# Who multiplies the one-hots of a key search, and another order in a cross-attention

## The reference, cut to what matters

```python
def memory_cross_attention(h, mem_n, wq, wkv, wo):      # 4 heads of 256, 256 memory rows
    ...
    sc = jnp.einsum('bshd,bmhd->bhsm', q, k)
    p = jax.nn.softmax(sc / math.sqrt(XA_HEAD_DIM), axis=-1)
    o = jnp.einsum('bhsm,bmhd->bshd', p, v)
    return o.reshape(b_, s_, D_MODEL) @ wo

def peer_ffn(x, wq, keys, u_tab, v_tab):                # 8 heads, 128 keys twice, 16384 experts
    q = (xt @ wq).reshape(t, PEER_HEADS, 2, HALF_Q)
    scores = jnp.einsum('thpd,hpnd->thpn', q, keys)
    s_top, i_top = lax.top_k(scores, PEER_TOPK)         # 16 of 128, for each head and half
    cand = (s_top[:, :, 0, :, None] + s_top[:, :, 1, None, :]).reshape(t, PEER_HEADS, 256)
    c_score, c_idx = lax.top_k(cand, PEER_TOPK)         # 16 of 256
    i1 = jnp.take_along_axis(i_top[:, :, 0], c_idx // PEER_TOPK, axis=-1)
    i2 = jnp.take_along_axis(i_top[:, :, 1], c_idx % PEER_TOPK, axis=-1)
    expert = i1 * N_KEYS + i2
    ...                                                 # gelu(x . u[expert]) * gate, then times v[expert]
```

## Time and profile before

| | us |
|---|---|
| median of 3 runs | 1758.8 |
| lowest and highest | 1757.88, 1760.15 |
| the profiled execution, whole | 1758.06 |
| its span, first to last instruction | 1756.3 |
| TensorE busy in it | 1695.2 |
| VectorE busy | 1173.5 |
| ScalarE busy | 932.6 |
| GpSimd busy | 134.0 |

### The profile page before, as it was taken

One profiled execution on the slowest core, in us unless ns is written; L12 is line 12 of the kernel. 1 busy time (PEld: TensorE's weight loads), 2 busy tenths in 40 slices (PEclk: granted clock), 3 DMA queues, 4 the chain that ended last, 5 costly groups with the idle time before them and its releaser, 6 DMA issues.

```text
span 1756.3 us, 30291 instructions
## 1 busy us (share of the span) xinstructions
PE 1695.2 (97%) x10344; PEld 1513.8 (86%) x10344; DVE 1173.5 (67%) x1753; ACT 932.6 (53%) x1536; POOL 134.0 (8%) x109
## 2 busy tenths in 40 slices
PE   7999999989998999999989989899999999999998
PEld 6888898889886788879889989899999988888887
DVE  5555787587654555467654899978888866666664
ACT  5445636476644444456444434456666655554454
POOL 0000004000000000010010020313222200000000
PEclk9999999989998999999999999999999999999999
DMA  7555544223552555544354446353444456555663
GB/s 258 188 182 183 173 169 153 99 96 133 168 170 94 169 189 182 191 157 160 118 188 147 168 143 191 132 166 134 143 139 136 155 179 192 193 192 193 194 194 121
DMA packets 78814, 286.79 MB, mean 163 GB/s; under 512 B 8864, under 2 KB 9120, under 8 KB 78624
## 3 DMA queue, kind: packets, MB, share of 16 engines
q1 hardware_dynamic: 77888, 282.27, 48.2%
q0 software_dynamic: 864, 3.67, 0.6%
HBM read 284.86 MB, written 1.05 MB: 163 GB/s over the span
## 4 chain that ended last, share of the span: by engine, by line
PE 85%; DVE 11%; ACT 3%; issue 1%; DMA 0%; POOL 0%; SPq 0%; ACTq 0%; DVEq 0%; POOLq 0%
PE ps L1698 25%; PE ps L1700 25%; PE ps L1699 25%; PE ps L2253 3%; DVE w_low L989 3%; DVE digit_hot L1593 1%; ACT w_high L483 1%; PE ps L1705 1%; PE ps L1787 1%; PE ps L2084 1%; DVE route L1598 0%; DVE xT_low L1023 0%; DVE tmp L1074 0%; ACT xn L499 0%; PE ps L2219 0%
## 5 line engine op out<-in xcount | busy, mean ns | idle before, releaser
L989 DVE TENSOR_TENSOR w_low<-ring,w_high 128x1024 fp32r<-128x1024 f32 x532 | 654.2, 1233 | 346.3 <-ACT w_high L483 344.4
L483 ACT ACTIVATE w_high<-ring 128x1024 fp32r<-128x1024 f32 x532 | 559.4, 1056 | 322.6 <-PE ps L1700 314.2
L1698 PE MATMUL ps<-xT_high,w_high 128*128 128x256 f32 x1600 | 463.5, 290 | 12.8 <-DVE w_low L989 10.7
L1699 PE MATMUL ps<-xT_high,w_low 128*128 128x256 f32 x1600 | 455.3, 285 | 0.0
L1700 PE MATMUL ps<-xT_low,w_high 128*128 128x256 f32 x1600 | 455.1, 284 | 0.0
L1698 PEld LDWEIGHTS ps<-xT_high,w_high 128*128 128x128 f32 x1600 | 309.7, 194 | 16.0 <-DVE w_low L989 14.0
L1699 PEld LDWEIGHTS ps<-xT_high,w_low 128*128 128x128 f32 x1600 | 309.8, 194 | 0.7 <-issue 0.5
L1700 PEld LDWEIGHTS ps<-xT_low,w_high 128*128 128x128 f32 x1600 | 309.3, 193 | 0.0
L1698 PE MATMUL ps<-w_high,expert_w_high 128*128 128x512 f32 x512 | 199.3, 389 | 0.0
L1699 PE MATMUL ps<-w_high,expert_w_low 128*128 128x512 f32 x512 | 199.2, 389 | 0.0
L1700 PE MATMUL ps<-w_low,expert_w_high 128*128 128x512 f32 x512 | 199.2, 389 | 0.0
(11 more groups left out here) (361 smaller groups left out, 2115.0 us busy)
## 6 DMA issues: line engine op xcount, KB each, us to landing
ring<-in_stream SPq DMA_DIRECT2D x532, 512.0 KB, 3.4
row_gain<-in_rows POOLq DMA_DIRECT2D x4, 512.0 KB, 4.4
h<-in_x SPq DMA_DIRECT2D x2, 512.0 KB, 4.0
mem_sb<-in_mem SPq DMA_DIRECT2D x1, 1024.0 KB, 11.4
keys_sb<-in_keys POOLq DMA_DIRECT2D x1, 1024.0 KB, 5.3
out<-result SPq DMA_DIRECT2D x2, 512.0 KB, 2.6
last_gain<-in_rows POOLq DMA_DIRECT2D x1, 512.0 KB, 5.6
cols<-in_cols SPq DMA_DIRECT2D x1, 78.5 KB, 7.2
```

The source lines that it names most:

```text
L483: act.activation(WH[:, n % SLOTS, :], RING[:, n % SLOTS, :], ACT.Copy).then_inc(w_high, 1)
L989: dve.tensor_tensor(WL[:, n % SLOTS, :], RING[:, n % SLOTS, :], WH[:, n % SLOTS, :].bitcast(F32), ALU.subtract).then_inc(w_split, 1)
L1698: pe.matmul(out, high, w_hi, start=start, stop=False, skip_group_check=True)
L1699: pe.matmul(out, low, w_hi, start=False, stop=False, skip_group_check=True)
```

## The change

In the cross-attention TensorE turns the probabilities between blocks 2 and 3 of kv3. The lower half goes to banks 2 and 3, the upper half to banks 6 and 7. After block 3 it waits for the lower half's copy alone, forms feature tiles 0 to 3 (banks 2 and 3), then waits for the upper half's copy and for kv3 out of PSUM, and forms tiles 4 to 7 (banks 0 and 1). The output product's first four blocks each wait only for the low part that they read. ScalarE and VectorE split two blocks of xa_o, copy their half of `xa_probsT`, split one, copy kv3 out, split the last.

In the key search the key numbers are kept as bfloat16 (`top_at_16`), VectorE itself multiplies both one-hots (line 1601 of the changed kernel), and sums them at once for either tt; GpSimd keeps only the fills. The gate subtraction moves ahead of the one-hots.

```diff
@@ gpsimd
-        for tt in range(TT):
-            if tt:
-                pool.wait_ge(tops_ok, 2)
-                pool.memset(GE[:, FIRST_GATED:80, :], 1.0).then_inc(slots_one, 1)
-            for p in range(2):
-                pool.wait_ge(hot_one, 2 * tt + p + 1)
-                hot = HOT[:, p, :, :].rearrange("p (h k) j -> p h k j", h=8)
-                pool.tensor_tensor(hot, hot, TOP_ATF[:, tt, p:16:2, :].unsqueeze(2).to_broadcast([P, 8, 16, 16]),
-                                   ALU.mult).then_inc(hot_ok, 1)
+        pool.wait_ge(tops_ok, 2)
+        pool.memset(GE[:, FIRST_GATED:80, :], 1.0).then_inc(slots_one, 1)
+        pool.wait_ge(hot_one, 4)
         pool.memset(GE[:, 80:105, :], 1.0).then_inc(slots_one, 1)
@@ scalar, cross-attention
-        split(BASE["xa_o"], 4)
+        split(BASE["xa_o"], 2)
+        act.wait_ge(xp_ps, 1)
+        act.activation(PT[:, 0:4, :], XP_PS[0], ACT.Copy).then_inc(xp_sb, 1)
+        split(BASE["xa_o"] + 2, 1)
         kv_evac(3)
-        act.wait_ge(xp_ps, 1)
-        act.activation(PT[:, 0:4, :], XT_PS[:, 0:4, :], ACT.Copy).then_inc(xp_sb, 1)
+        split(BASE["xa_o"] + 3, 1)
@@ vector, cross-attention
-        split(BASE["xa_o"], 4)
+        split(BASE["xa_o"], 2)
+        dve.wait_ge(xp_ps, 2)
+        dve.tensor_copy(PT[:, 4:8, :], XP_PS[1]).then_inc(xp_upper, 1)
+        split(BASE["xa_o"] + 2, 1)
         kv_evac(3)
-        dve.wait_ge(xp_ps, 2)
-        dve.tensor_copy(PT[:, 4:8, :], XT_PS[:, 4:8, :]).then_inc(xp_sb, 1)
+        split(BASE["xa_o"] + 3, 1)
@@ vector, key search
+            dve.tensor_tensor(gate_of(tt), CTOP[:, tt, :, :], CTOP[:, tt, :, 0:1].to_broadcast([P, 8, 16]),
+                              ALU.subtract).then_inc(gd_ok, 1)
             if tt:
                 dve.wait_ge(hot_used, 2 * tt)
             for p in range(2):
...
                                   ALU.is_equal).then_inc(hot_one, 1)
                 tick(long=True)
+            for p in range(2):
+                dve.wait_ge(hot_one, 2 * tt + p + 1)
+                hot = HOT[:, p, :, :].rearrange("p (h k) j -> p h k j", h=8)
+                dve.tensor_tensor(hot, hot, TOP_AT16[:, tt, p:16:2, :].unsqueeze(2).to_broadcast([P, 8, 16, 16]),
+                                  ALU.mult).then_inc(hot_ok, 1)
+            tick(long=True)
+            keys_of(tt)
@@ tensor, cross-attention
-        kv_panel(3, range(1, 4))
-        kv_out(3)
+        kv_panel(3, range(1, 3))
         for half in range(2):
             for h in (2 * half, 2 * half + 1):
                 for tt in range(TT):
...
             last.then_inc(xp_ps, 1)
-        pe.wait_ge(xp_sb, 2)
+        kv_panel(3, range(3, 4))
+        pe.wait_ge(xp_sb, 1)
         for ft in range(8):
+            if ft == 4:
+                pe.wait_ge(xp_upper, 1)
+                kv_out(3)
...
+        for kt in range(4):
+            pe.wait_ge(xo_low, kt // 2 + 1)
+            rows_product("xa_o", 8, range(kt, kt + 1))
         pe.wait_ge(xo_low, 4)
-        rows_product("xa_o", 8, range(4))
```

More of the change, by code:

```diff
@@ L121, in build @@
     KV_PAIR = [PAIR[1], PAIR[1], PS[:, 2048:3072], PAIR[0]]
+    XP_PS = [p.rearrange("p (k t) -> p k t", k=4) for p in (PAIR[1], PS[:, 3072:4096])]
+    XO_PS = [PS[:, b * 512:(b + 1) * 512] for b in (2, 3, 0, 1)]
     IDENT = sb("ident", [P, P], 64)
@@ L208, in build @@
     HOT = sb("digit_hot", [P, 2, 128, 16], 64.5, BF16)
-    TOP_ATF = sb("top_at_f", [P, TT, 16, 16], 72.5)
+    TOP_AT16 = sb("top_at_16", [P, TT, 16, 16], 72.5, BF16)
     CTOP = sb("cand_top", [P, TT, 8, 16], 74.5)
@@ L313, in build @@
     xs_sc, xs_max, xs_exp, xs_norm = sem("xa_scores"), sem("xa_max"), sem("xa_exp"), sem("xa_norm")
+    xp_upper = sem("xa_probsT_upper_ok")
     xp_ps, xp_sb, xo_ps, xo_high, xo_low = (sem("xa_probsT_psum"), sem("xa_probsT_ok"), sem("xa_o_psum"),
@@ L770, in _ @@
             act.activation(HTH[:, 2 * bank:2 * bank + 2, :],
-                           PS[:, 2048 + bank * 512:2560 + bank * 512].rearrange("p (k t) -> p k t", k=2),
-                           ACT.Copy).then_inc(xo_high, 1)
+                           XO_PS[bank].rearrange("p (k t) -> p k t", k=2), ACT.Copy).then_inc(xo_high, 1)
         act.preload_act_table_set("sqrt_and_others")
@@ L1363, in _ @@
             k2 = slice(2 * bank, 2 * bank + 2)
-            dve.tensor_tensor(HTL[:, k2, :], PS[:, 2048 + bank * 512:2560 + bank * 512].rearrange("p (k t) -> p k t", k=2),
+            dve.tensor_tensor(HTL[:, k2, :], XO_PS[bank].rearrange("p (k t) -> p k t", k=2),
                               HTH[:, k2, :].bitcast(F32), ALU.subtract).then_inc(xo_low, 1)
@@ L1565, in keys_of @@
         def keys_of(tt):
-            dve.wait_ge(hot_ok, 2 * tt + 2)
             for p in range(2):
+                dve.wait_ge(hot_ok, 2 * tt + p + 1)
                 dve.reduce_sum(ROUTE[:, tt, p, :], HOT[:, p, :, :], AX_X).then_inc(hot_used, 1)
@@ L1576, in _ @@
             dve.wait_ge(injected, 1)
-            dve.tensor_copy(TOP_ATF[:, tt, :, :], TOP_AT[:, tt, :, :]).then_inc(tops_ok, 1)
+            dve.tensor_copy(TOP_AT16[:, tt, :, :], TOP_AT[:, tt, :, :]).then_inc(tops_ok, 1)
             chain(dve.tensor_tensor(CAND[:, tt, :, :].rearrange("p h (a b) -> p h a b", a=16),
@@ L1596, in _ @@
                 tick(long=True)
-            dve.tensor_tensor(gate_of(tt), CTOP[:, tt, :, :], CTOP[:, tt, :, 0:1].to_broadcast([P, 8, 16]),
-                              ALU.subtract).then_inc(gd_ok, 1)
-        keys_of(1)
+            for p in range(2):
[5 more added lines that the diff above has]
+            keys_of(tt)
         split(b + PB + ticks[1], STEP0 - ticks[1])
@@ L2077, in _ @@
                     for mt in range(2):
-                        last = pe.transpose(XT_PS[:, 2 * h + mt, tt * P:(tt + 1) * P],
+                        last = pe.transpose(XP_PS[half][:, 2 * h + mt - 4 * half, tt * P:(tt + 1) * P],
                                             PE_[:, tt, h, mt * P:(mt + 1) * P], IDENT[:])
             last.then_inc(xp_ps, 1)
-        pe.wait_ge(xp_sb, 2)
+        kv_panel(3, range(3, 4))
+        pe.wait_ge(xp_sb, 1)
         for ft in range(8):
+            if ft == 4:
+                pe.wait_ge(xp_upper, 1)
+                kv_out(3)
             for mt in range(2):
-                last = pe.matmul(PS[:, 2048 + ft * SEQ:2048 + (ft + 1) * SEQ],
+                last = pe.matmul(XO_PS[ft // 2][:, ft % 2 * SEQ:(ft % 2 + 1) * SEQ],
                                  XAV[:, ft // 4, mt, ft % 4 * P:ft % 4 * P + P], PT[:, ft // 2 * 2 + mt, :],
```

2 lines of the change are left out of this document (removed).

## The result

| | before | changed |
|---|---|---|
| median, us | 1759.5 | 1731.1 |
| lowest and highest, us | 1757.88, 1762.31 | 1729.96, 1734.61 |
| executions | 4 | 4 |
| the profiled execution, us | 1758.06 | 1730.03 |
| mean granted clock in it | 0.985 | 0.991 |

The ratio is 0.984, with a 95% interval from 0.982 to 0.9861: 1.6% faster. Predicted were 1734.1 us, range 1730.5 to 1741.0.

The account below looks back on a forecast made before the run. TensorE, busy 1695.2 of 1756.3 us, bounds the kernel; only its idle and half-clock time can be won. Key search 16.0 plus cross-attention 8.7 gives 24.7 us: 1758.8 - 24.7 = 1734.1, range 1730.5 to 1741.

Parts of the forecast that it names:

- The search, 16.0 us: Key search: without GpSimd's multiplies holding VectorE, idle time and half clock together win 16.0 us, at worst 12.7.
- The multiply, taken from the split's row: Key search: VectorE's new bfloat16 multiply costs 1.15 us net, like a split, within a span of 1.2 to 2.3.
- The row of line 1013: Profile row of 1024 elements in a mean of 0.76 us, cited to show VectorE can do two elements per cycle.
- the sum's 2.27: Key search: VectorE's sum reads 2048 bfloat16 numbers in 2.27 us, cited for a slow multiply.
- The account of the lead: Key search: VectorE's lead over TensorE's need, split by split, falls from 5.9 to 0.4 us: no stall, but barely.
- The slow multiply's price: Key search rival, chance 0.12: multiply as slow as the one-hot, 1.7 us stall a pass, 3.3 in both, 1737.4 us.
- The feared half clock: Key search: half clock following the slow multiply's stalls would cost 1.3 us more a pass, 1740.0 us.
- The cross-attention, 8.7 us: Cross-attention: product starts 11.6 us after block 2 of kv3, winning 8.7 us: three gaps (5.8) and 2.9 of half clock.
- the listed waits: Cross-attention: possible waits for normalisation, copies, kv3 out of PSUM, low parts or a load; moved-wait rival chance 0.05, 1737.2 us.
- The 2.9 of half clock: Cross-attention: the part of the 8.7 us gain that comes from half clock rather than the three gaps.
- its forecast: Whole kernel: 1734.1 us, given chance 0.68 for 1731 to 1736.5, as half-clock stretches elsewhere may shift by some us.
- the last gap 1.41 us: Cross-attention: third TensorE gap, 1.41 us, before the output product, counted among the three gaps to be won.

Follow-up runs that it names:

- e2: The kernel before with the key search's part of the change alone, old cross-attention kept: 1740.39 us, ratio 0.9905.
- e3: The changed kernel with the key numbers kept in fp32 instead of bfloat16: 1735.69 us, ratio 0.9871 against the kernel before.
- e8: The kernel before with 12 unread matmuls in TensorE's 3.10 us gap ahead of the cross-attention's transposes: 1756.38 us, ratio 0.9984.
- e9: The changed kernel itself, unchanged, run again as neighbour on another chip: ratio 0.9848 against the kernel before, executions 1730.21 to 1735.46 us.
- e7: The changed kernel, but the cross-attention's output product waits for all four low parts at once: ratio 0.9873 against the kernel before.
- e10: The changed kernel, output product again waiting for all four low parts at once, run a second time: ratio 0.9872 against the kernel before.
- e12: The changed kernel plus an unrelated GpSimd multiply of two fp32 operands beside VectorE's sums in the search: 1736.88 us in one execution.

## Why the prediction was right, point by point

- **The search, 16.0 us: 16.1 measured** by split starts, 16.0 alone in e2. The cause was read rightly: an instruction of VectorE held to GpSimd's end. That it is the two SBUF operands that count was not in the prediction; it had only seen that the sum in the earlier trace rows was not slowed, and used that for the fill, rightly.
- **The multiply, taken from the split's row, 1.15 net: 1.13** (2.35 for two, less the overlap). The row of line 1013 and the packed split were the right neighbours, the sum's 2.27 the wrong one. The width of the operands decides: with the key numbers alone in fp32 the multiply takes 2.28 (e3).
- **The account of the lead** came out step for step. The need is 0.14 us before a Gelu, as in e3, where the block before the first stall ends at 1034.58 and the Gelu starts at 1034.72. In the changed kernel the split behind the first multiplies ends at 1029.93 and the need is 1031.35 - 0.14 = 1031.21: lead 1.3, as predicted. The last one ends at 1036.58 against 1036.97: 0.4, as predicted.
- **The slow multiply's price, 1.7 in a pass: 2.05 measured** (e3). Lateness was 0.9 instead of 0.8 and each sum added 0.46 as supposed; what was missing is the restart, 1.14 lost for a gap of 0.9 (the third bullet of the last section). The feared half clock didn't follow.
- **The cross-attention, 8.7 us: 9.2.** Of the 11.6 us the stage took 11.2, since 16 transposes take 1.67 net (517.28 to 518.95) and not 2.0, the block of kv3 2.85 (to 521.80) instead of 2.7, and the values 6.71 (to 528.51) instead of 6.9. None of the listed waits came true. The 2.9 of half clock among the 8.7 is 2.6 by e8.
- **What was missed** of the 28.0 us in the profiled pair are 28.0 - 24.7 = 3.3: 0.5 in the cross-attention, 0.5 between it and the search, 0.1 in the search, and 2.4 ahead of everything that the change touches, less 0.2 behind it. The prediction had allowed for these on either side, in a range of 1731 to 1736.5 for its forecast, and the median of 1731.1 just lies in it. The early 2.4 are luck: e9, the same kernel, has a median of 1734.6, 0.5 above the forecast. The effect of the change itself is best taken from the local gains, 9.2 + 0.5 + 16.1 = 25.8 us, 1.1 more than predicted; e9's median is 25.5 under that of the kernel before beside it.
- **A cost that was not seen at all** is that of the single wait in front of the output product. I had priced the low parts by the time the product needs them, which is right for the changed kernel, and called the last gap 1.41 us. The traces of e7 and e10 put the cost of leaving it at some 5 us, most of it further on, as much as 360 us later.

## What to carry to other kernels

Before an operation is shared out to GpSimd, look at what VectorE has to do meanwhile. In these runs a GpSimd multiply, which reads SBUF, held every VectorE instruction with two SBUF operands that came up until it ended, and an operation that costs VectorE 1.2 us itself is cheaper there than the 3.9 us of standing. Keep an account of the lead of a feeding engine, split by split: here it told a lead of 0.4 us to a tenth before the change was made. Where half-clock stretches differ from execution to execution, compare kernels stage by stage: the medians of two sets of four and five executions of one kernel lie 3.5 us apart.

## What the runs showed of the hardware that was not expected

- The granted clock of TensorE fell to 0.50 in e7 and e10 near 820 us although TensorE had been busy without a gap for 59 us. Just before, it works through short matmuls (27 in the 2 us before the level falls in e7). The changed kernel works through the same matmuls there, also without a gap, and its level stays at 1.00. A gap is not the only thing in front of a half-clock stretch. Against the changed kernel e7 and e10 have only the wait of 1.4 us, some 290 us earlier. Neither being later nor such a wait does it by itself: e9 reaches the place 5.3 us after the changed kernel's first profile and keeps 1.00, and so does the kernel before, which has a gap of 1.41 us there as well. Why the level falls is open.
- The length of the half clock at one place differs between executions of the same program: 3.4 us near 255 in the first profile of the changed kernel, 10.2 in the second. The time moves by 3.1 us with it, and by another 1.1 with the stretch near 367 us (10.2 instead of 6.8).
- A wait of 0.90 us cost TensorE 1.14 (e3). The first matmul behind it takes 0.38 us where its neighbours take 0.28, which is 0.1 of the rest. Most of what is left is how the gap is counted: the neighbours start 0.12 us apart and are counted for 0.28, and this overlap of 0.16 is missing at the wait too.

```profile
1035.48 0.38 PE L1702 MATMUL ps<-xT_high,w_high 128*128 128x256 f32 x1 [0.90 <-DVE w_low L988]
1035.70 0.28 PE L1703 MATMUL ps<-xT_high,w_low 128*128 128x256 f32 x1
```

- GpSimd's multiply of 2048 elements takes 5.0 us with bfloat16 operands and with one fp32 operand alike; with two of fp32, 5.5. In each of these rows it starts while VectorE is in a two-operand instruction, and part of its duration may be its own waiting: in e12 it starts at 1033.47 while the split runs to 1034.52. With that time taken off, some 4.5 us are left for e12 and 4.0 for the others, which is an estimate.
